# Hybrid attention and DeltaNet block: another division of the input norm among the engines, and another order of weight splits and stores in the projection

## What is computed

```python
h = rms_norm(x, norm_mix_g[l])          # y = x * rsqrt(mean(x^2) + eps) * g
proj = h @ w_in[l]
(qa, ka, va, qi, ki, wi, qb, kb, vb, zb, bb, ab) = jnp.split(proj, SPLIT_POINTS, axis=-1)
...
qkv = jax.nn.silu(causal_depthwise_conv(jnp.concatenate([q, k, v], axis=-1), conv_w))
```

## Time and profile before

| what | value |
|---|---|
| median of three runs | 3744.95 us (3734.8 to 3747.73) |
| the profiled execution | 3748.16 us, its span 3746.4 us |
| TensorE busy | 3338.0 us, 89% |
| VectorE, ScalarE, GpSimd busy | 2115.7 (56%), 2162.7 (58%), 1376.2 us (37%) |
| first stage: last eviction starts | 485.74 us |
| mean granted TensorE clock | 0.953 of full |

### The profile page before, as it was taken

One profiled execution on the slowest core, in us unless ns is written; L12 is line 12 of the kernel. 1 busy time (PEld: TensorE's weight loads), 2 busy tenths in 40 slices (PEclk: granted clock), 3 DMA queues, 4 the chain that ended last, 5 costly groups with the idle time before them and its releaser, 6 DMA issues.

```text
span 3746.4 us, 47222 instructions
## 1 busy us (share of the span) xinstructions
PE 3338.0 (89%) x16770; PEld 2756.5 (74%) x16770; DVE 2115.7 (56%) x3680; ACT 2162.7 (58%) x3717; POOL 1376.2 (37%) x721
## 2 busy tenths in 40 slices
PE   7899968888889995689999889999889999989998
PEld 5678857777767884567787668788677878867886
DVE  5223126777987863656546575758576575444223
ACT  4222127676856553587886869696877944433232
POOL 3111134335354533324444334343323333334443
PEclk9999989999999997799999999999999999999999
DMA  3521153513334444323333433334343333342322
GB/s 117 202 79 73 68 143 65 136 52 91 82 99 97 96 128 125 98 83 120 98 114 120 122 115 104 118 113 119 99 127 116 107 105 103 97 129 86 100 96 79
DMA packets 282665, 395.44 MB, mean 106 GB/s; under 512 B 22832, under 2 KB 204208, under 8 KB 277808
## 3 DMA queue, kind: packets, MB, share of 16 engines
q1 hardware_dynamic: 277680, 360.97, 33.0%
q10 hardware_dynamic: 4752, 31.46, 2.1%
HBM read 320.61 MB, written 71.73 MB: 105 GB/s over the span
## 4 chain that ended last, share of the span: by engine, by line
PE 28%; ACT 15%; DVE 9%; issue 5%; POOL 2%; DMA 1%; SPq 0%; ACTq 0%; DVEq 0%; POOLq 0%
PE m_ps L2105 8%; PE m_ps L2106 7%; PE m_ps L2107 7%; ACT m_junk L1806 6%; ACT m_wh L1870 2%; PE m_ps L2208 2%; PE m_ps L2190 2%; POOL m_wl L1749 2%; ACT m_prob L1897 1%; ACT m_verdict L1808 1%; ACT m_trial L1812 1%; ACT m_phi L1886 1%; PE m_ps L2175 1%; PE m_ps L2176 1%; DVE m_rl L1945 1%
## 5 line engine op out<-in xcount | busy, mean ns | idle before, releaser
L1749 POOL TENSOR_TENSOR m_wl<-m_raw,m_wh 128x1024 fp32r<-128x1024 f32 x288 | 719.7, 2499 | 1327.3 <-ACT m_wh L1870 1327.3
L2105 PE MATMUL m_ps<-m_ah,m_wh 128*128 128x512 f32 x1280 | 523.8, 409 | 25.4 <-DVE m_al L1962 18.0
L2107 PE MATMUL m_ps<-m_ah,m_wl 128*128 128x512 f32 x1280 | 506.2, 395 | 0.0
L2106 PE MATMUL m_ps<-m_al,m_wh 128*128 128x512 f32 x1280 | 505.7, 395 | 0.0
L2105 PE MATMUL m_ps<-m_th,m_wh 128*128 128x512 f32 x1024 | 415.3, 406 | 16.9 <-DVE m_tl L1947 10.1
L2107 PE MATMUL m_ps<-m_th,m_wl 128*128 128x512 f32 x1024 | 404.5, 395 | 0.0
L2106 PE MATMUL m_ps<-m_tl,m_wh 128*128 128x512 f32 x1024 | 404.1, 395 | 0.0
L1806 ACT ACTIVATE m_junk<-m_sc,m_trial 128x1152 int8<-128x1152 f32 (+7 forms) x248 | 401.5, 1619 | 2.2 <-DVE m_sc L2065 1.1
L1870 ACT ACTIVATE m_wh<-m_raw 128x1024 fp32r<-128x1024 f32 x288 | 302.8, 1051 | 147.6 <-PE m_ps L2107 139.3
L1945 DVE TENSOR_TENSOR m_rl<-m_rl 128x512 f32<-128x512 f32 x128 | 104.5, 816 | 361.0 <-ACT m_th L1826 360.5
L2105 PEld LDWEIGHTS m_ps<-m_ah,m_wh 128*128 128x128 f32 x1280 | 244.8, 191 | 80.1 <-DVE m_al L1962 20.2
(11 more groups left out here) (321 smaller groups left out, 7499.7 us busy)
## 6 DMA issues: line engine op xcount, KB each, us to landing
m_raw<-w_units SPq DMA_DIRECT2D x288, 512.0 KB, 3.5
m_vals<-valsT SPq DMA_DIRECT2D x240, 128.0 KB, 3.5
p_raw<-w_proj SPq DMA_DIRECT2D x72, 256.0 KB, 4.5
m_rot<-rowsQ SPq DMA_DIRECT2D x50, 256.0 KB, 4.9
projT<-work ACTq DMA_DIRECT2D x12, 1024.0 KB, 3.8
g_qkvz<-projT SPq DMA_DIRECT2D x16, 768.0 KB, 5.4
wraw<-w_proj SPq DMA_DIRECT2D x21, 512.0 KB, 3.6
work<-xT SPq DMA_DIRECT2D x8, 1024.0 KB, 5.6
```

Source lines behind the costliest of these rows:

```text
L1749: nc.gpsimd.tensor_tensor(wl[:, n % 3, :], raw[:, n % 2, :], wh[:, n % 3, :].bitcast(fp32), ALU.subtract).then_inc(w_lo, 1)
L2105: nc.tensor.matmul(dst, hi, rh, start=first, stop=False)
L2106: nc.tensor.matmul(dst, hi, r_low, start=False, stop=False)
L2107: return nc.tensor.matmul(dst, lo, rh, start=False, stop=last)
```

## The change

Four things change in the first stage.

1. The sum of squares. VectorE adds the 8 pieces of squares down to 2 (`sum_squares` on VectorE: one add of 1024 columns, one of 512, into `xsum`), and TensorE sums the two with two matmuls instead of eight (four instructions in the trace).
2. The homes of x. Instead of two buffers `xb` and two buffers `xn` there are five homes, in which x lands, is scaled in place and is read for both parts. A load waits only for a home to be done with (`xl_done`); the first five wait for nothing.
3. The low part of x is made by VectorE (`lower`), one block behind the scale, and no longer by GpSimd, which keeps the low parts of the weights.
4. On ScalarE the code of a chunk is cut in two, `evacuate` and `give_out`. The split of weight chunk c+2 stands right behind the evictions of chunk c, and SiLU and store of a convolved chunk stand behind the evictions of the chunk after it. On TensorE, chain 4 follows the sum of block 7 as before.

```diff
-        xb = work[:, 0:4096].rearrange("p (u k s) -> p u k s", u=2, k=KC)
-        xn = [a.rearrange("p (k s) -> p k s", k=KC) for a in (work[:, 6144:8192], stage[:, 1, HALO:HALO + KC * XB])]
+        x_homes = [work[:, 0:2048], work[:, 2048:4096], work[:, 6144:8192], stage[:, 1, HALO:HALO + KC * XB],
+                   stage[:, 0, HALO:HALO + KC * XB]]
+        xb = [a.rearrange("p (k s) -> p k s", k=KC) for a in x_homes]
...
-                if b >= 2:
-                    sp.wait_ge(xn_done, b - 1)
-                sp.dma_start(xb[:, b % 2, :, :], xT[:, :, tokens(b)]).then_inc(x_in[b % 2], 16)
+                if b >= NH:
+                    sp.wait_ge(xl_done, b - NH + 1)
+                sp.dma_start(xb[b % NH], xT[:, :, tokens(b)]).then_inc(x_in[b % NH], 16)
...
             w_load(0)
+            x_load(2)
             w_load(1)
-            for b in range(2, NX):
+            for b in range(3, NX):
                 x_load(b)
...
-            for b in range(NX):
-                pool.wait_ge(xh_done, b + 1)
-                nc.gpsimd.tensor_tensor(normed(xl, b), xn[b % 2], normed(xh, b).bitcast(fp32),
-                                        ALU.subtract).then_inc(xl_done, 1)
-            for c in range(2, N):
+            for c in range(N):
                 split_lo(c)
...
+            def sum_squares(b):
+                dve.wait_ge(sq_done, b + 1)
+                if b >= 2:
+                    dve.wait_ge(ss_done, b - 1)
+                st.do(nc.vector.tensor_tensor(xsq[:, 0:4, :], xsq[:, 0:4, :], xsq[:, 4:8, :], ALU.add))
+                nc.vector.tensor_tensor(xsum[:, b % 2, :, :], xsq[:, 0:2, :], xsq[:, 2:4, :], ALU.add).then_inc(sum_done, 1)
...
+            def lower(b):
+                dve.wait_ge(xh_done, b + 1)
+                nc.vector.tensor_tensor(normed(xl, b), xb[b % NH], normed(xh, b).bitcast(fp32), ALU.subtract).then_inc(xl_done, 1)
+
+            sum_squares(0)
+            for b in range(NX):
+                scale(b)
+                for x in ahead(b):
+                    sum_squares(x)
+                if b:
+                    lower(b - 1)
+            lower(NX - 1)
...
+            act.wait_ge(xl_done, NH)
...
+            for c in range(N):
+                evacuate(c)
+                if c + 2 < N:
+                    split_hi(c + 2)
+                if c and kinds[c - 1][0] == "conv":
+                    give_out(c - 1)
+                if kinds[c][0] != "conv":
+                    give_out(c)
...
-                for k in range(KC):
-                    last = nc.tensor.matmul(ps[:, ss_bank(b), 0:XB], ones[:, :], xsq[:, k, :], start=(k == 0), stop=(k == KC - 1))
+                for half in range(2):
+                    last = nc.tensor.matmul(ps[:, ss_bank(b), 0:XB], ones[:, :], xsum[:, b % 2, half, :], start=(half == 0), stop=(half == 1))
```

More of the change, by code:

```diff
@@ L100, in norm_and_projection @@
         rstd = sb("rstd", [P, 2, XB])
+        xsum = sb("xsum", [P, 2, 2, XB])
         ones = sb("ones", [P, P])
@@ L111, in norm_and_projection @@
         pair = lambda n: [sem(f"{n}{u}") for u in range(2)]
-        x_in, w_in = map(pair, ["x_in", "w_in"])
+        x_in, w_in = [sem(f"x_in{u}") for u in range(NH)], pair("w_in")
         split_kept, shared_in = sem("split_kept"), sem("shared_in")
-        sq_done, ss_done, log_done, rstd_done, xn_done, xh_done, xl_done = map(
-            sem, ["sq_done", "ss_done", "log_done", "rstd_done", "xn_done", "xh_done", "xl_done"])
+        sq_done, sum_done, ss_done, log_done, rstd_done, xn_done, xh_done, xl_done = map(
+            sem, ["sq_done", "sum_done", "ss_done", "log_done", "rstd_done", "xn_done", "xh_done", "xl_done"])
         w_hi, w_lo = map(sem, ["w_hi", "w_lo"])
@@ L120, in norm_and_projection @@
         tokens = lambda b: slice(b * XB, (b + 1) * XB)
+        ahead = lambda b: [b + 1] if b + 1 < NX else []
         block = ctx.enter_context(nc.Block())
@@ L183, in _, with scale @@
             st = Steps(dve, dve_s)
+            def sum_squares(b):
[4 more added lines that the diff above has]
+                nc.vector.tensor_tensor(xsum[:, b % 2, :, :], xsq[:, 0:2, :], xsq[:, 2:4, :], ALU.add).then_inc(sum_done, 1)
             dve.wait_ge(const_in, 32)
-            for b in range(NX):
+            def scale(b):
                 dve.wait_ge(rstd_done, b + 1)
-                if b >= 2:
-                    dve.wait_ge(xl_done, b - 1)
                 for k in range(KC):
                     last = nc.vector.scalar_tensor_tensor(
-                        out=xn[b % 2][:, k, :], in0=xb[:, b % 2, k, :], scalar=gm[:, k:k + 1], in1=rstd[:, b % 2, :],
+                        out=xb[b % NH][:, k, :], in0=xb[b % NH][:, k, :], scalar=gm[:, k:k + 1], in1=rstd[:, b % 2, :],
                         op0=ALU.mult, op1=ALU.mult)
                 last.then_inc(xn_done, 1)
+            def lower(b):
[9 more added lines that the diff above has]
+            lower(NX - 1)
             for k in range(N_CONV):
@@ L212, in square @@
             def square(b):
-                act.wait_ge(x_in[b % 2], 16 * (b // 2 + 1))
+                act.wait_ge(x_in[b % NH], 16 * (b // NH + 1))
                 if b:
-                    act.wait_ge(ss_done, b)
-                nc.scalar.activation(xsq[:, :, :], xb[:, b % 2, :, :], ACT.Square).then_inc(sq_done, 1)
+                    act.wait_ge(sum_done, b)
+                nc.scalar.activation(xsq[:, :, :], xb[b % NH], ACT.Square).then_inc(sq_done, 1)
             def split_hi(c):
@@ L234, in _, with evacuate @@
                 nc.scalar.activation(rstd[:, b % 2, :], rstd[:, b % 2, :], ACT.Exp, scale=-0.5).then_inc(rstd_done, 1)
[L235 to L238, removed]
+                for x in ahead(b)[:1]:
+                    square(x)
+                if b == 0:
+                    split_hi(0)
                 act.wait_ge(xn_done, b + 1)
-                nc.scalar.activation(normed(xh, b), xn[b % 2], ACT.Copy).then_inc(xh_done, 1)
-            for c, (kind, chunk, k, blocks) in enumerate(kinds):
+                nc.scalar.activation(normed(xh, b), xb[b % NH], ACT.Copy).then_inc(xh_done, 1)
+                if b == 1:
+                    split_hi(1)
+                for x in ahead(b)[1:]:
+                    square(x)
+            act.wait_ge(xl_done, NH)
+            def evacuate(c):
+                kind, _, _, blocks = kinds[c]
                 u = c % 2
-                if 1 <= c < N - 1:
-                    split_hi(c + 1)
                 if c >= 2:
@@ L254, in _, with give_out @@
                                          ACT.Silu if kind == "z" else ACT.Copy).then_inc(evac_done, 1)
+            def give_out(c):
+                kind, chunk, k, blocks = kinds[c]
+                u = c % 2
                 if kind == "conv":
@@ L296, in _ @@
                 sum_squares(b)
-                if b >= 3:
+                if 3 <= b < NX - 1:
                     project(b - 3)
-            for n in range(NX - 3, len(chains)):
+            for n in range(4, len(chains)):
                 project(n)
```

5 lines of the change are left out of this document (2 added, 3 removed).

## The result

The changed kernel takes 3707.79 us in the median of four runs (3701.33 to 3711.39), the kernel before 3745.28; the ratio is 0.9904, with a 95% interval from 0.9886 to 0.9921. By the medians 37.5 us are gone, by the interval 30 to 43. The profiled execution took 3707.24 us, with a span of 3705.4.

What follows compares the result with a forecast made beforehand. TensorE, busy 89% of the span, bounds the kernel. Gains of 11.4 (norm's head), 2.7 (low x) and 23.1 us (ScalarE order) sum to 37.2: 3711.0 from the profiled execution, 3707.7 from the median; forecast 3709, range 3697 to 3720.

Steps and rivals of the forecast that it cites:

- The account of before: First stage from 85.84 to 485.7: 373.05 us of chains plus 26.8 us of waits and slow restarts (19.2 + 2.7 + 4.9).
- The order on ScalarE: At the index chunks, earlier weight splits remove 19.2 us of waits and 4.9 of restarts, less 1.0: gain 23.1 us.
- Rival 2: At the index chunks, GpSimd gets the port only after all four convolution ops: 16.3 us less gain, 3727; chance 0.05.
- The norm's head: In the norm, chain 4 starts at about 74.4, gain 11.4 us; the 2.7 us wait for low x goes too.
- Rival 1: In the norm, VectorE's low part or adds cost nearer GpSimd's price: chain 4 at 84, gain 27, 3720; chance 0.08.
- rival 3: Norm's head: clock stays at 0.50 for chains 0 to 3, 5.3 us more each: 3729; chance 0.03, going on 0.02.
- The sum: Whole first stage: 11.4 + 2.7 + 23.1 = 37.2 us gained.

Runs made afterwards that it cites:

- experiment 6: Changed kernel with three of the four VectorE operations left out for convolved chunks 0 and 2; last eviction at 446.78, GpSimd's low weights 2.40 us.
- experiment 3: Changed kernel with the low part of x on GpSimd again; median 3715.18 us, ratio 0.9921.
- experiment 4: Changed kernel with eight matmuls per block on TensorE instead of the two adds and two matmuls; median 3711.45 us, ratio 0.9909.

## Why the prediction was right, point by point

**The account of before.** That two waits and the slower restarts behind them cost 24 us, and the norm the rest, is borne out: the order alone brings 21.2 us, the norm alone 13.2. One reading was slightly off: the prediction lets chain 4 start where the eighth sum's last matmul is shown to end, at 85.84; by the timeline it starts at 85.49.

**The order on ScalarE, 23.1 us.** It measured 21.2 alone (464.54): 22.3 gained from chain 4 on, and 1.1 lost ahead of it in that execution. The chain of times T+... came out as worked: with T the end of chain 7 at about 97.9, the chunk's last eviction is at 97.94, the second low weights start at 99.57, the third at 105.07 (T+7.2, foreseen T+7.1 to 7.2) and end at 108.90 (T+11.0, foreseen T+11.3). TensorE waits 0.16 and 0.18 us; I had booked 0.5 each. Rival 2, GpSimd held up by a whole convolution, is refuted by that row and by experiment 6: it was one instruction. The rule of the Trainium skill (SBUF — State Buffer, Who interferes with whom), that whichever starts first keeps the port for its whole instruction, agrees with the 3.83 and 2.40 us. The 3.80 us at 17.24 fit it less plainly: by the rows GpSimd's op starts 0.38 us before VectorE's first add and still ends 2.2 us after it, so that it would have been passed by an instruction that started later. Spans on GpSimd are rough, and this was not tested.

**The norm's head, 11.4 + 2.7 us.** Chain 0 at 41.51 (foreseen 41.75), rstd of block 7 at 74.1 (74.0), chain 4 at 74.28 (74.4). That it is right to 0.2 us is partly luck, since two errors cancel. Block 4's rstd was there at 50.1, 1.5 us earlier than foreseen (51.65), and the three periods behind it took 24.0 us instead of 22.35, because the middle one was 9.36: the sum of block 6 stood on TensorE behind chain 2, which was slow (next paragraph but one), and VectorE waited 2.04 us for rstd. In the two other profiles of the changed kernel chain 4 starts at 74.73 and 73.77. Smaller errors: the low part took 2.28 us, not 2.35, the second add 0.69, not 0.62; the scale of block 2 started at 32.95, not 34.0. Rival 1, the dear low part, falls by the same rows. The wait of 2.7 us is gone; experiment 3 brings back 2.4 of it.

**Which part of the norm carried it.** The prediction gave the head one sum. Taken out of the changed kernel one by one, the low part on VectorE is worth 11 us or more, two of the five homes 17 us or more, the adds 1 to 3. These are not shares of one gain: they add up to more than twice the 13.2 us of the norm alone. With three homes the changed norm is slower than the one of before (chain 4 at 92.59 against 85.49): a home scaled in place is held until its low part is made, where before a load waited only for the scale. The five homes are what lets the rest work. The adds I had booked on both sides, 1.85 us on VectorE and 2.7 us off TensorE, but not what a block costs without them. By experiment 4 that is 8.9 to 9.05 us instead of 7.3 to 9.4, and chain 0 is 0.9 us earlier, so that chain 4 is only 2.3 us later.

**The clock.** This is the part that came out otherwise than foreseen. Chain 0 was to start on the lower clock and fill 7.5 to 8.4 us. The granted clock is recorded as 1.00 there, yet its first six matmuls took as long as those of a chain at 0.50: in the timeline the first pair below is chain 0, the second pair chain 2, where the granted clock was 0.50 from 57.63 to 60.90. They start 0.42 to 0.43 us apart, where 0.23 is usual.

```profile
42.08 0.63 PE L325 MATMUL ps<-xl,wh 128*128 128x512 f32 x1
42.50 0.63 PE L326 MATMUL ps<-xh,wl 128*128 128x512 f32 x1
...
58.62 0.63 PE L326 MATMUL ps<-s_xh,wl 128*128 128x512 f32 x1
59.05 0.63 PE L324 MATMUL ps<-s_xh,wh 128*128 128x512 f32 x1
```

So chain 0 did start slowly. It filled 6.6 us (41.51 to 48.14), less than foreseen, and 7.0 and 7.5 in the two other profiles. What failed was the argument that waits of a microsecond leave the clock alone: it fell in chain 2 and chain 4. The changed kernel by stretches (busy of PE, PEld, DVE, ACT, POOL, then clock, DMA share, GB/s; the first holds chain 0 and the sum behind it):

```profile
41.51:48.80 7.29, 7.29 (x28) 5.98 (x29) 6.48 (x11) 4.43 (x4) 0.00 (x0) 1.00 0.45 144
...
57.63:65.30 7.67, 7.67 (x27) 6.18 (x28) 7.12 (x11) 3.52 (x2) 0.00 (x0) 0.78 0.34 126
...
71.42:74.28 2.86, 1.13 (x4) 0.70 (x5) 2.86 (x3) 1.50 (x3) 0.00 (x0) 1.00 0.00 0
...
74.28:81.60 7.32, 7.32 (x25) 5.90 (x26) 7.32 (x10) 2.89 (x3) 0.00 (x0) 0.77 0.00 0
```

Ahead of chain 4 TensorE had done 1.13 us of work in 2.86, and the chain then ran in part at 1.2 GHz, 7.15 us (to 81.43) instead of 5.5; chain 2 filled 7.2. It is rival 3 in its short form, in two chains instead of four and for 1.7 us each, not 5.3. It is also not the same in every execution: in the second profile of the changed kernel only chain 2 was slow and chain 4 took 5.54 us (74.73 to 80.27), in the third neither was (5.7 and 5.6 us, at 1.00), though TensorE waited about 0.7 and 1.2 us ahead of chain 2 in all three. What decides it is not shown. From chain 4 to the last eviction it is 375.6 us in the first profile and 374.0 in both others. The loop that the Trainium skill describes (TensorE: Matmul & The Clock Gate, HAM oscillation) is not this one: its waits are 3 to 5 us long and put the clock down each time. The prediction let that passage speak for rival 3, whose waits are of 1 us; what it says of long waits did not bear on them.

**The sum.** 37.2 us foreseen. In the profiles the first stage gave 35.9 (and 37.1 and 38.0 in the two later ones), the medians differ by 37.5. In parts: the start of chain 4 was to come 11.4 us earlier and came 11.2, 10.8 and 11.7; from chain 4 to the last eviction 25.8 us were to go (2.7 + 23.1), and 24.7, 26.3 and 26.3 went. The first profile's 41.0 us flatter the change by 5 us of the second stage.

## What to carry to other kernels

When GpSimd and VectorE both work on-chip data, count GpSimd's op on VectorE's account too: moving 4.5 us of GpSimd work to VectorE, where it takes 2.3, made VectorE's block shorter. In an in-order queue put what another engine needs next directly behind the event that frees it, and what nobody awaits behind that; and follow a buffer's release through the queue it stands in, not only through its semaphore. To compare versions a few microseconds apart, compare the start of the next stage behind a barrier: in three profiles of the changed kernel it lay within 2.1 us, where their spans (3705.4, 3706.2, 3697.0) lay 9 us apart. Even so, a difference of 3 us needs more than one profile of each.

## What the runs showed that was not expected

- The second stage, unchanged in all of them, took from 956.2 to 968.2 us in the fourteen profiles, and the third from 2287.8 to 2298.5. Of the difference of 5.3 us between the first two profiles 2.8 us are there by the 13th of the stage's 16 stores to `mixT` (issued 816.5 and 819.3 us from the stage's start), and 5.4 by the 14th (876.1 and 881.5). In the last quarter the mean granted clock is 1.00 in the shorter and 0.98 in the longer one:

```profile
1200.00:1413.90 213.90, 195.27 (x1172) 1.00 0.41 111
```

```profile
1236.20:1455.40 219.20, 200.61 (x1181) 0.98 0.40 108
```

(stretches of TensorE alone: length, busy, clock, DMA share, GB/s; the changed kernel and the kernel before). Stretches of equal length can't tell where a difference arises, since all that is left over falls into the last one. What decides it was not tested.

- Matmuls at a granted clock of 1.00 can still be slow after idling: the four of a sum took 2.07 us at 29.89, and 1.13 when chains surround them. The first matmuls of chain 0 are another case (above). So the time between two matmuls is to be read beside the granted clock.

- A small store can be slow behind large ones. ScalarE's store of an index chunk was issued at 113.40, right behind a 1 MB store on the same queue (113.03), while 4 MB of xh and xl went out from 109.30 on, and the next eviction into its buffer waited for it until 128.09:

```profile
128.09 1.09 ACT L275 ACTIVATE stage<-ps 128x512 f32<-128x512 f32 x2 [11.88 <-DMA projT<-stage]
```

TensorE did not wait for it: the bank in question was wanted later still.
